# A mixture-of-experts decoder kernel: the router's bias row fetched at the start, and a later wait for half of an expert's tokens

## The reference, cut to what matters

```python
u = rms_norm(h, m_pre_norm)
logits = (tok @ router_w) + router_b                  # tok is (256, 1024), router_b has 8 numbers
probs = jax.nn.softmax(logits, axis=-1)
top_p, top_i = lax.top_k(probs, TOP_K)                # TOP_K = 2
top_p = top_p / jnp.sum(top_p, axis=-1, keepdims=True)
gate = jnp.sum(jax.nn.one_hot(top_i, N_EXPERTS) * top_p[..., None], axis=1)
for ex in range(N_EXPERTS):                           # w_gate_up (1024, 7168), w_down (3584, 1024)
    y = y + gate[:, ex:ex + 1] * swiglu(tok, w_gate_up[ex], w_down[ex])
h = h + rms_norm(y, m_post_norm)
```

## Time and profile before

| | |
|---|---|
| median of 3 executions | 1352.91 us (1350.77 to 1357.46) |
| the profiled execution's own time | 1353.34 us |
| its span, first to last instruction | 1351.4 us |
| PE busy | 1290.0 us, 95% of the span |
| DMA moved | 424.34 MB |

### The profile page before, as it was taken

The page is one execution under the profiler, slowest core; times in us unless marked ns, Lnnn a source line. Parts: engine busy times, 40 slices in busy tenths (PEclk is TensorE's granted clock), DMA queues, the critical chain, the costliest instruction groups (busy, mean ns, idle before and its releaser), DMA issues.

```text
span 1351.4 us, 26213 instructions
## 1 busy us (share of the span) xinstructions
PE 1290.0 (95%) x11388; PEld 744.0 (55%) x11388; DVE 422.1 (31%) x807; ACT 347.6 (26%) x660; POOL 50.6 (4%) x77
## 2 busy tenths in 40 slices
PE   8989999999889989999999999999999989999986
PEld 7988999999788873443343443333443332343331
DVE  7785866653697731001010001000001000000102
ACT  7886544443567630000000000000000000000001
POOL 3001100001120010000000000000000000000000
PEclk9999999999999979999999999999999999999999
DMA  9538455555223398999999999999999999999994
GB/s 288 166 97 265 127 186 183 162 185 161 69 96 110 116 376 320 356 366 397 417 418 418 416 417 419 416 418 419 415 417 419 416 418 419 416 418 418 417 418 186
DMA packets 128133, 424.34 MB, mean 314 GB/s; under 512 B 8321, under 2 KB 77185, under 8 KB 99345
## 3 DMA queue, kind: packets, MB, share of 16 engines
q1 hardware_dynamic: 127664, 421.58, 80.4%
q0 software_dynamic: 352, 1.06, 0.2%
HBM read 421.56 MB, written 1.05 MB: 313 GB/s over the span
## 4 chain that ended last, share of the span: by engine, by line
PE 70%; SPq 13%; DMA 7%; DVE 5%; ACT 3%; issue 2%; DVEq 0%; POOL 0%; ACTq 0%
PE bank L934 29%; SPq L1058 12%; PE bank L911 10%; PE bank L530 9%; PE bank L532 8%; PE bank L531 8%; DMA ring_low<-in_m_w_gate_up 4%; DMA ring_low<-in_m_w_down 2%; PE bank L889 1%; PE bank L870 1%; PE bank L901 1%; PE bank L903 1%; DMA rbias<-in_gain_rows 1%; DVE w_lo L1579 1%; ACT w_hi L1181 1%
## 5 line engine op out<-in xcount | busy, mean ns | idle before, releaser
L934 PE MATMUL bank<-ring_low,x_T 128*32 128x512 f32 (+1 forms) x3552 | 344.1, 541 | 9.4 <-DMA ring_low<-in_m_w_gate_up 8.1
L934 PEld LDWEIGHTS bank<-ring_low,x_T 128*32 128x32 f32 x3552 | 113.3, 110 | 234.3 <-issue 210.5
L911 PE MATMUL bank<-ring_low,eT 128*32 128x512 f32 x1632 | 182.4, 594 | 11.9 <-DMA ring_low<-in_m_w_down 11.9
L530 PE MATMUL bank<-u_hi,w_hi 128*128 128x272 f32 (+1 forms) x568 | 166.4, 293 | 7.0 <-DVE u_lo L1634 5.1
L1579 DVE TENSOR_TENSOR w_lo<-raw,w_hi 128x2048 fp32r<-128x2048 f32 (+7 forms) x89 | 143.9, 1638 | 93.6 <-ACT w_hi L1181 93.4
L532 PE MATMUL bank<-u_hi,w_lo 128*128 128x272 f32 (+1 forms) x568 | 164.2, 289 | 0.0
L531 PE MATMUL bank<-u_lo,w_hi 128*128 128x272 f32 (+1 forms) x568 | 163.5, 288 | 0.0
L2072 DVE TENSOR_TENSOR e_h<-bank,e_h 128x512 f32<-128x512 f32 (+1 forms) x40 | 22.7, 618 | 416.9 <-PE bank L934 416.9
L934 PE MATMUL bank<-ring_high,x_T 128*32 128x384 f32 (+1 forms) x1568 | 149.8, 536 | 0.0
L1181 ACT CAST w_hi<-raw 128x2048 fp32r<-128x2048 f32 (+7 forms) x89 | 117.9, 1352 | 52.9 <-PE bank L532 52.9
L911 PEld LDWEIGHTS bank<-ring_low,eT 128*32 128x32 f32 x1632 | 50.1, 110 | 135.1 <-issue 111.9
(11 more groups left out here) (321 smaller groups left out, 1353.0 us busy)
## 6 DMA issues: line engine op xcount, KB each, us to landing
ring_low<-in_m_w_gate_up SPq DMA_DIRECT2D x92, 1024.0 KB, 23.1
ring_low<-in_m_w_down SPq DMA_DIRECT2D x80, 1024.0 KB, 23.8
ring_low<-in_m_w_gate_up SPq DMA_DIRECT2D x88, 768.0 KB, 22.0
ring_high<-in_m_w_gate_up SPq DMA_DIRECT2D x36, 1024.0 KB, 24.5
ring_high<-in_m_w_down SPq DMA_DIRECT2D x32, 1024.0 KB, 24.7
ring_high<-in_m_w_gate_up SPq DMA_DIRECT2D x40, 768.0 KB, 21.8
raw<-in_f_w_gate_up SPq DMA_DIRECT2D x24, 1024.0 KB, 5.3
raw<-in_f_w_down SPq DMA_DIRECT2D x12, 1024.0 KB, 5.2
```

The source lines that it names most:

```text
L530: nc.tensor.matmul(o, a[0], b[0], start=start, stop=False)
L911: return nc.tensor.matmul(strip(q, t, NT), eT[u][:, bank, P * i + GROUP * at:P * i + GROUP * at + GROUP], w[:, n, :], start=start, stop=stop)
L934: last = nc.tensor.matmul(strip(q + 3 * (kind_of == "up"), t, width), x_T[:, part, group(g)], w[:, width * n:width * n + width], start=(pa ...
```

## The change: where the bias row is fetched, and where PE waits for the second half of the tokens

`rbias` gets a place of its own in memory from the start, ahead of the weight buffers, which moves most tiles by 32 bytes. Its fetch becomes POOL's first instruction. The semaphore `in_rows` is split in `in_bias` (router) and `in_grow` (waited for by DVE after the expert loop). On PE the wait for `x_by_dve` goes from the expert's piece 0 to its piece 4.

```diff
+        rbias = sb("rbias", [P, NE])
         banks = [ctx.enter_context(nc.psum_tensor(f"bank{i}", [P, 512], F32)) for i in range(8)]
...
-        rbias = sb("rbias", [P, NE])
...
                         if c == 0:
                             pe.wait_ge(x_by_act, ex * 4 + 4)
-                            pe.wait_ge(x_by_dve, ex * 4 + 4)
                             if kind == BIG:
                                 pe.wait_ge(scatter_added, it * 4 + 4)
+                        if c == 4:
+                            pe.wait_ge(x_by_dve, ex * 4 + 4)
...
+            pool.dma_start(rbias[:], gain_rows[0:1, D:D + NE].to_broadcast([P, NE])).then_inc(in_bias, 16)
             pool.wait_ge(in_par, 16)
             pool.wait_ge(dve_step, 2)
...
             at(pool, "chunk", CH[("b_out", 3)])
-            pool.dma_start(grow[:], gain_rows[0:1, 0:D].to_broadcast([P, D])).then_inc(in_rows, 16)
-            pool.dma_start(rbias[:], gain_rows[0:1, D:D + NE].to_broadcast([P, NE])).then_inc(in_rows, 16)
+            pool.dma_start(grow[:], gain_rows[0:1, 0:D].to_broadcast([P, D])).then_inc(in_grow, 16)
...
-            dve.wait_ge(in_rows, 32)
+            dve.wait_ge(in_bias, 16)
             dve.wait_ge(h_summed, 2 * NB)
...
+            dve.wait_ge(in_grow, 16)
+
             def with_gain(i):
```

More of the change, by code:

```diff
@@ L397, in yoco_kernel @@
         hi_done, lo_done = sem("hi_done"), sem("lo_done")
-        in_const, in_par, in_rows, in_ident = sem("in_const"), sem("in_par"), sem("in_rows"), sem("in_ident")
+        in_const, in_par, in_bias, in_grow, in_ident = (
+            sem("in_const"), sem("in_par"), sem("in_bias"), sem("in_grow"), sem("in_ident"))
         in_x = [sem(f"in_x{b}") for b in range(3)]
```

## The result

The changed kernel took 1338.42 us (median of 4, 1337.20 to 1339.03) where the kernel before took 1351.84 (median of 4, 1349.32 to 1357.46). The ratio is 0.9894 with a 95% interval of 0.9861 to 0.9927. The profiled execution took 1338.85 us, its span is 1337.0 where before it was 1351.4.

What follows compares the result with a forecast made beforehand. The saturated weight stream, started by the first expert on PE, was taken to bound the kernel; 2.05 + 1.2 - 0.1 = 3.15 us off 1353.34 gave 1350.2 us, range 1345.5 to 1354.5.

Steps and rivals of the forecast that it cites:

- the tiles' places: Weight stream: moving `ring_low` by 32 bytes, from 224 to 0 past a multiple of 256, taken at nothing.
- the rule: Weight stream: part-used transactions for descriptors off a 256-byte boundary; sum an estimated 15 us lower, left out of the forecast.
- Faster, by the new places: Rival, weight stream: 2.7% off some 580 us by `ring_low`'s new place, 15.7 us, giving 1334.5; chance 0.04.
- Part one: Router: bias row there from the start, bias addition at the logits' end, count right behind the filler; gain 2.05 us.
- Part two: First expert on PE: wait for DVE's half moved to piece 4, start some 0.06 us after the gather; gain 1.2 us.
- The early fetch: Kernel's start: 4 KB bias fetch beside first tokens and weights; cost 0.1 us taken, bounds nothing and 1.7.
- The fast gather: Rival, gather before the first expert: clock stays up, another 3.42 us, giving 1346.8; chance 0.22, partly fast included.
- the gain reaches the end: Weight stream: an earlier first expert starts saturation earlier, last piece about 3.2 us earlier; rival of unchanged 1353.3, chance 0.12.

Runs made afterwards that it cites:

- f3_low224_high0: Kernel before with `ring_high` at 0 past a multiple of 256, `ring_low` left at 224; one execution, 1347.39 us against 1355.6.
- the stream alone: Two kernels without compute, only fetching weight pieces to chosen places past a multiple of 256; 427 to 428 GB/s all at 0, 421 all at 224.
- f2_wait_at_0: Changed kernel with PE's wait for DVE's half of the tokens back at piece 0; one execution, 1344.76 us against 1355.6.
- g1_after_again: Changed kernel run once more, unaltered, beside its variants on one chip; 1340.67 us against 1354.88 for the kernel before, ratio 0.9906.
- f1_late_fetch: Changed kernel with the bias fetch moved back in POOL's stream, behind the store of `gain_row`; 1341.30 us against 1355.6, ratio 0.9900.

## Why the prediction was wrong

**The step that failed** is the one on the tiles' places: "417 and 416 GB/s. I take nothing for it." The measurement was right and the reading wrong. It compared `ring_low` at 224 past with `ring_high` at 64 past, two bad places, which alone reach 421 and 423 GB/s. The test was also too blunt, as the same two windows of the changed kernel show, in which one tile is at 0 past and the other at 64:

```profile
744.00:756.00 12.00, 12.00 (x132) 5.21 (x128) 2.58 (x4) 1.17 (x2) 0.00 (x0) 1.00 1.02 423
756.00:768.00 12.00, 12.00 (x156) 4.85 (x152) 0.00 (x0) 1.25 (x3) 0.00 (x0) 1.00 1.01 423
```

They are equal again, and 6 to 7 GB/s above those of before. Only with `ring_high` as the one good place (`f3_low224_high0`) do they differ, 419 and 424. Two tiles in one queue can run alike and both be slow, or both be fast. No row of before showed a piece at a multiple of 256, so equal rates could not speak about moving to one. The rows bounded the difference between two bad places only; the unknown cost of a good one should have been left open down to the figure of the rule. Measured, the term that was put at nothing is 11.6 us between first piece and last landing. The rival "Faster, by the new places" had the right mechanism, and 4% of the chance; its 15.7 us was too much.

**The rule.** The Trainium skill, "DMA: Bandwidth & Descriptors", section "How a descriptor splits into AXI transactions", was set aside. It says that a descriptor (here one row of a piece) whose start is not a multiple of 256 costs extra, and the runs agree. It tells of bytes fetched in vain before the start; here the place that changed was the one written to, and the runs show a cost there. The estimate of 2.7% from its beats at 224 past was too large: over the whole ring that is 1.9% (15.7 us of 825), where the loop lost 1.4%, and in the stream alone all pieces at 224 past lost 1.4%. By its beats 32 past should cost an estimated 0.4%; alone, 32 past cost as much as 224, 6 of 427 GB/s. The runs show a step and hardly a slope, with 421 at 32 and 224 past and 423 at the five places between.

**Part one** was right in its mechanism: the addition at the logits' end, the filler as the next thing late, the count behind it. From the logits' end to the count it took 5.68 us before and 3.39 now, 2.29 less where 2.05 was forecast. The 5.68 is one draw: the seven profiles with the fetch in its old place have 3.46 to 5.94, as it landed early or late (8.6 to 10.4 us from issue), while the seven with the fetch moved and both filler matmuls have 3.38 or 3.39. From the count to the gather 1.58 us was taken as unchanged; it took 1.82, the count's products now running at a granted clock of 0.50.

**Part two** was right: PE's gap of 1.26 us is gone in the first profile and back in `f2_wait_at_0`, and a wait for `x_T` at piece 4 appears in no row.

**The early fetch** was mis-sized: 0.1 taken, about 0.9 measured at the head and at the logits' end, within the bounds of 0 and 1.7. The choice went by bytes. At the head ACT waits for the tokens (2.17 us idle on them in the changed kernel, 1.16 before), so any delay of theirs counts at once; why 4 KB delay them by 0.9 us is not shown.

**The fast gather** was rightly a rival with a smaller share. Of the seven profiles with the fetch moved and both filler matmuls, none of which has the hole in PE's work, five had a gather of 6.7 to 6.8 us and two one of 3.78. An eighth, `f3_low224_high0`, has no hole either, since its fetch landed early, and a gather of 7.03. What decides between them was not found. In `g1_after_again` it stood as follows, and its span was 1333.5, 3.5 us under the first profile of the same kernel:

```profile
492.62 3.71 PE L639 MATMUL bank<-con 128*128 128x512 f32 x4
...
497.64 3.78 PE L833 MATMUL bank<-sel,u_tok 128*128 128x96 f32 x32 [0.52 <-DVE sel L1974]
501.35 1.92 PE L936 MATMUL bank<-ring_low,x_T 128*32 128x512 f32 x16
```

and the chain's last transfer, 3.5 us before that of the first profile:

```profile
1294.02 24.61 DMA ring_low<-in_m_w_down
```

**That the gain reaches the end** was right: an earlier first piece shifted the saturated stream with it. In seven profiles with the same places the first piece starts anywhere from 501.35 to 507.20, and the last landing follows 817.1 to 817.3 us later in each.

## What to carry to other kernels

When an edit adds, drops or moves a tile, read where the tiles behind it land, before anything else: a stream of transfers that sets the time ran 1.2 to 1.7% faster into a tile at a multiple of 256 bytes, whatever the edit was for. A row that shows no difference between two cases says nothing of a third that it does not contain; a rule of the Trainium skill that covers just that third case keeps its chance. And a fetch is not free for being small: ask what arrives at the same time and who waits for it.

## What the runs showed that was not expected

- One good row in two is enough: pieces at 0 and 224 past in turn ran at 427 GB/s, as all at 0. In runs as long as the ring's it is nearly enough: 5 of 17 places at 64 past cost the changed kernel at most 1 GB/s, or about 1 us of the loop.
- 64 past a multiple of 256 is no better in a stream of its own kind than 96, 128, 160 or 192 (423 each); 32 and 224 had 421.
- The time outside the span differs: 1353.34 - 1351.4 = 1.9 us in the first profile of before, 1341.38 - 1336.4 = 5.0 in `f1_late_fetch`. It is 1.8 to 2.1 us or 4.9 to 5.7 in every execution whose span is on record, both for the same kernel, and nothing between. What looks like a chip's own pace lies largely there: the medians of before in the last four comparisons spread over 2.5 us, the medians of their spans only over 0.8 (1350.9 to 1351.7). The spans compare better than the times where effects of 1 us matter, and stretches within them better still.
